# Pair attention: the second head of each pair is normalized on GpSimd, the first on VectorE

## The reference

```
s = q k^T / 8   (+ window mask and sink in layer 0)
p = exp(s - max) / sum(exp(s - max))
o = p v
```

## Time and profile before

| what | us |
|---|---|
| median of three runs | 2543.71 (2541.72 to 2549.36) |
| the profiled execution | 2542.04 |
| its span | 2540.2 |
| TensorE, matmul busy | 2137.8 (84%) |
| VectorE busy | 1087.4 (43%) |
| ScalarE busy | 681.5 (27%) |
| GpSimd busy | 262.3 (10%) |

### The profile page before, as it was taken

One profiled execution on the slowest core, in us unless ns is written; L12 is line 12 of the kernel. 1 busy time (PEld: TensorE's weight loads), 2 busy tenths in 40 slices (PEclk: granted clock), 3 DMA queues, 4 the chain that ended last, 5 costly groups with the idle time before them and its releaser, 6 DMA issues. The chain is left out here.

```text
span 2540.2 us, 29357 instructions
## 1 busy us (share of the span) xinstructions
PE 2137.8 (84%) x11338; PEld 1358.5 (53%) x11338; DVE 1087.4 (43%) x1713; ACT 681.5 (27%) x1048; POOL 262.3 (10%) x392
## 2 busy tenths in 40 slices
PE   6889999996999997987979888888568698888884
PEld 5777787784777876764733333333355433333331
DVE  5667644545676545467531111111576411111112
ACT  3343434332333432246211011111316111111111
POOL 2010000100000000000211111111120111111110
PEclk9989999997999998999979999999779799999997
DMA  8745565551655646310489999999810889999994
GB/s 278 266 144 203 181 211 191 202 200 67 236 199 182 217 173 216 110 35 1 189 354 396 409 413 406 410 404 382 276 25 1 311 356 408 422 415 413 413 414 188
DMA packets 175984, 655.24 MB, mean 258 GB/s; under 512 B 17680, under 2 KB 63200, under 8 KB 150544
## 3 DMA queue, kind: packets, MB, share of 16 engines
q1 hardware_dynamic: 157888, 618.45, 63.7%
q0 software_dynamic: 16752, 32.20, 3.9%
q10 hardware_dynamic: 1248, 3.25, 0.3%
HBM read 653.64 MB, written 21.17 MB: 266 GB/s over the span
## 5 line engine op out<-in xcount | busy, mean ns | idle before, releaser
L651 PE MATMUL bank<-sb_ring_rounded,sb_hT_rounded 128*128 128x512 f32 x2672 | 675.5, 397 | 18.9 <-DVE sb_hT_rounded L1727 12.2
L1185 PE MATMUL bank<-sb_ring,sb_arena 128*64 128x512 f32 x1984 | 507.4, 659 | 129.5 <-DMA sb_ring<-in_w_up 126.7
L651 PEld LDWEIGHTS bank<-sb_ring_rounded,sb_hT_rounded 128*128 128x128 f32 x2672 | 506.0, 191 | 128.5 <-DVE sb_hT_rounded L1727 14.1
L1740 DVE TENSOR_TENSOR sb_ring_rounded<-sb_ring,sb_ring_rounded 128x2048 fp32r<-128x2048 f32 (+1 forms) x148 | 328.2, 2259 | 133.1 <-ACT sb_ring_rounded L1295 132.8
L1185 PEld LDWEIGHTS bank<-sb_ring,sb_arena 128*64 128x64 f32 x1984 | 155.9, 150 | 426.4 <-issue 418.9
L1295 ACT ACTIVATE sb_ring_rounded<-sb_ring 128x2048 fp32r<-128x2048 f32 (+1 forms) x148 | 271.7, 1886 | 171.1 <-PE bank L651 141.8
L651 PE MATMUL bank<-sb_ring_rounded,sb_arena_rounded 128*128 128x512 f32 x1168 | 312.5, 393 | 2.0 <-DVE sb_arena_rounded L1727 1.0
L651 PEld LDWEIGHTS bank<-sb_ring_rounded,sb_arena_rounded 128*128 128x128 f32 x1168 | 221.1, 190 | 48.8 <-issue 2.6
L1209 PE MATMUL bank<-sb_ring,sb_arena 128*64 128x512 f32 x1024 | 233.7, 598 | 1.7 <-DVE sb_arena L2458 1.7
L1643 ACT ACTIVATE sb_hb<-bank 64x512 f32<-64x512 f32 x64 | 37.8, 590 | 644.6 <-PE bank L1185 644.6
L2458 DVE COPY sb_arena<-bank 128x256 f32<-128x256 f32 x64 | 27.2, 425 | 396.1 <-PE bank L1196 396.0
(11 more groups left out here) (315 smaller groups left out, 1955.0 us busy)
## 6 DMA issues: line engine op xcount, KB each, us to landing
sb_ring<-in_w_down SPq DMA_DIRECT2D x64, 2048.0 KB, 22.8
sb_ring<-in_w_up SPq DMA_DIRECT2D x62, 2048.0 KB, 21.8
sb_ring<-in_w_gate SPq DMA_DIRECT2D x62, 2048.0 KB, 17.5
sb_ring<-in_w_ada SPq DMA_DIRECT2D x48, 1024.0 KB, 7.4
sb_ring<-in_ffn_w_gu SPq DMA_DIRECT2D x44, 1024.0 KB, 7.7
sb_ring<-in_xa_w_kv SPq DMA_DIRECT2D x16, 1024.0 KB, 7.3
sb_ring<-in_ffn_w_down SPq DMA_DIRECT2D x16, 1024.0 KB, 6.4
sb_ring<-in_od_w_in SPq DMA_DIRECT2D x12, 1024.0 KB, 6.3
```

The costliest lines, as they stand in the source:

```text
L651: ins = pe.matmul(bank[b][0:rows, :], rnd(x), rnd(w[:, k, :]), start=start and k == k0 and q == 0, stop=stop and k == k1 - 1 and q == len( ...
L1185: ins = pe.matmul(bank[2 * j + part][part * ROWS:(part + 1) * ROWS, :], mxT[:, j, k, :], w[:, k, :], start=k == 0, stop=k == KD - 1)
L1740: dve.tensor_tensor(rnd(w), w, whole(high_of(n)[:, k0:k1, :]), ALU.subtract).then_inc(*c.up(s["w_lo"]))
```

## The change

VectorE inverts the sums as before, with a semaphore of its own (`inv_ready`), waits for its own result, and scales head 0 only, raising `p_ready`. GpSimd gets a loop over the same steps: it waits for `inv_ready`, scales head 1 in place and raises `p1_ready`. TensorE waits for both before the transposes of a pair. Two semaphores are added.

```diff
                         pe.wait_ge(*c.next(s["p_ready"]))
+                        pe.wait_ge(*c.next(s["p1_ready"]))
                         claim(T0)
...
-                        step(dve.reciprocal(inv, total))
-                        for a in range(2):
-                            e = j_e[:, m % 2, a, 0:nk]
-                            ins = dve.tensor_scalar(e, e, inv[:, a:a + 1], None, ALU.mult)
-                            if a == 0:
-                                ins.then_inc(*c.up(s["dve_step"]))
-                        ins.then_inc(*c.up(s["p_ready"]))
+                        dve.reciprocal(inv, total).then_inc(*c.up(s["inv_ready"]))
+                        dve.wait_ge(*c.last())
+                        e = j_e[:, m % 2, 0, 0:nk]
+                        dve.tensor_scalar(e, e, inv[:, 0:1], None, ALU.mult).then_inc(*c.up(s["p_ready"]))
...
+                for m, (t, i) in enumerate(pair_steps(l)):
+                    e, q = j_e[:, m % 2, 1, 0:len(key_tiles(t)) * P], 2 * (m % 2)
+                    pool.wait_ge(*c.next(s["inv_ready"]))
+                    pool.tensor_scalar(e, e, st[:, 29 + q:30 + q], None, ALU.mult).then_inc(*c.up(s["p1_ready"]))
                 tiles = 4 - 2 * l
                 pool.wait_ge(*c.next(s["o_split"]))
```

More of the change, by code:

```diff
@@ L175, in build_program @@
             "act_back", "act_go", "act_step", "ctx_loaded", "bcx", "o_split", "dve_step", "e_ready",
-            "es_ready", "fin_ready", "gla_dve", "h_ready", "idx_ready", "logits_read", "in_loaded",
+            "es_ready", "fin_ready", "gla_dve", "h_ready", "idx_ready", "inv_ready", "p1_ready", "logits_read", "in_loaded",
             "marks_ready", "fix_loaded", "mem_loaded", "mod_stored", "raw_stored0", "raw_stored1", "silu_ready", "ms_ready", "mul_ready", "nmax_ready", "out_done",
```

## The result

The changed kernel takes 2569.46 us (median of four runs, 2568.06 to 2576.57); the kernel before takes 2545.32 us beside it (four runs, 2541.72 to 2549.36). The ratio is 1.01, with a 95% interval of 1.0081 to 1.012: slower by 24.1 us. I had forecast 2545.8, with a range up to 2556.

What follows compares the result with a forecast made beforehand. A loop of waits between VectorE and TensorE in pair attention was taken to set the pace; +0.8 (layer 0, four tiles), +1.8 (layer 1) and -0.5 us (two tiles) gave +2.1, so 2545.8 us, range 2539 to 2556.

Steps and rivals of the forecast that it cites:

- the three stretches: Pair attention: layer 0 over four and two key tiles, layer 1 over four; 166 us where any microsecond reaches the end.
- the hold: GpSimd's scaling waits until VectorE's, taken as first, ends at 0.69 us after the reciprocal starts.
- d: Lateness of TensorE's transposes after the reciprocal's start: p - 0.53 = 0.37 us over four key tiles, 0.14 over two.
- VectorE's saving: One scaling fewer per VectorE iteration: 0.40 us over four key tiles, 0.27 over two, only where VectorE sets the iteration.
- halves of four tiles above 8.3 us: Sign of being wrong: two pairs over four key tiles taking longer than this; halves near 7.8 and 6.9 us were expected.
- p: GpSimd's time to scale one head of 128x512: 0.90 us, between 0.53 and 1.29 or 1.82; 0.54 for 256 columns.
- the rule quoted there: VectorE tensor_scalar in a two-port mode and GpSimd share ports; the first to issue keeps them for the whole instruction.
- 18p - 14.1: Total change in us over the pair attention as a function of GpSimd's price; +2.1 forecast, +9.1 at 1.29, +18.6 at 1.82.
- the clock: Rival: more TensorE idling brings one more part at 1.2 GHz, 1 to 3 us each; clock or something else 0.03.
- GpSimd slow: Rival, chance 0.16: GpSimd's price alone decides from 1.21 us on; 2552.8 us at 1.29, 2562.3 at 1.82.
- GpSimd first: Rival, chance 0.14: GpSimd's scaling gets hold first, VectorE's ends 0.36 us later; +8.4 us in all, 2552.1.
- No conflict: Rival, 0.12 together with a price near the lower bound: both scalings run at once; -3.2 us, 2540.5.

Runs made afterwards that it cites:

- two_sems: Against the changed kernel: VectorE scales both heads again, each with its own semaphore, TensorE waiting for both ahead of the transposes; 2545.86 us, stretches 108.31 and 58.86 us.
- pool_both: Against the changed kernel: GpSimd scales both heads, VectorE none; 2617.22 us in one execution, GpSimd's scaling 1.562 us for 512 columns.
- one_port: Against the changed kernel: VectorE scales head 0 in the slower form that also sums its row; 2574.16 us in one execution, GpSimd's scaling 1.566 us.
- between_dve: Against the kernel before: VectorE scales both heads, a semaphore each, TensorE's wait for head 1 between the two heads' transposes; 2541.68 us, ratio 0.9982.

## Why the prediction was wrong

**Right:** the place and the mechanism. The time went into the three stretches. VectorE came first, its scaling unchanged; the handover left GpSimd's record 0.06 us behind it; the hold was 0.29 us (0.31 in the sum: the 0.44 left of VectorE's scaling less 0.13). The second wait costs nothing, as two_sems shows. In the settled halves, those at the lower clock apart, d is added to the loop's half to 0.1 us, and VectorE's saving is worth 0.20 us in the one half over two tiles that it sets, and nothing over four. I had named halves of four tiles above 8.3 us as a sign of being wrong; they are 8.47.

**Wrong:** the term p. "One input read and one output written lies between the write-only and the two-input row; I take the middle, p = 0.90 us". Measured by itself it is 1.565 us for 512 columns and 0.925 for 256. It is more than the two-input row makes with a fixed part (1.29), so the order in which I had put the three kinds was wrong, and the middle had nothing to stand on. Why this scaling costs more than the operation on two inputs would at that width, no run shows. The Trainium skill's 769 ns for 512 elements (GPSIMD Engine Reference, section 3.1) is for a best case; against this operation it is half of what was measured. The true value lay between my own upper bounds of 1.29 and 1.82; the range left out the higher one. The lower bound was also worked out wrongly: 1.823 us over 2048 columns is 0.89 ns a column, or 0.80 beyond a fixed 0.18 us, and gives 0.59 us and not 0.53. That moves the middle by 0.03 us and decides nothing.

A reading of the earlier trace rows was too strong. The prediction says that the trace agrees at both places with the rule quoted there. But at 508.50 VectorE runs a tensor_tensor and not a tensor_scalar, and at 1267.01 the engine recorded first was the one held. The two places show that one engine can hold the other, not that the first one does.

With p = 1.565 my line 18p - 14.1 gives +14.1 us. Measured at equal clock it is 16.2; the sum's other terms are good to some 2 us. The line would have given a median of 2557.8. The 11.7 us that are missing to 2569.46 are these 2, about 5 of the clock, 1.6 by which the kernel before has a higher median beside it than alone (2545.32 against 2543.71), and 3 that stay open with the parts outside the stretches. These parts rest on few traces; only the first 14.1 are worked out from the loop.

**Too small:** the clock. "More idle could bring one more such part, at 1 to 3 us each" stood under the rivals with 0.03. It is some 5 us on average. It goes with the lateness, though not in every execution: in layer 0 the granted clock was 0.91, 0.94 and 0.88 in the three traces of the changed kernel, 0.94, 0.94 and 0.98 in those of the kernel before, and 0.80 in pool_both, where the transposes are latest. Why equal executions differ in it is open.

So the rival *GpSimd slow*, with a chance of 0.16, was what happened, though its price is 1.565, and with that price the loop gives 2557.8; of the rest, which carried the median beyond even that rival's upper end of 2562.3, the lower clock is the largest part that I can name. *GpSimd first* did not occur; forced, it gave something else than it said. *No conflict* is refuted by the hold that one_port takes away.

## What to carry to other kernels

When an operation inside a loop of waits goes to another engine, count from the moment the inputs are ready to the moment the consumer can go on; that VectorE becomes free sooner is worth nothing if it waits in the same loop. A price that the trace does not show is not to be interpolated between rows of other operations: let the range reach both bounds, or give the rival at the upper bound more chance. If the second half of a pair is late, put the wait for it between the halves: with both on VectorE, that was the only part of this change that gained (between_dve, 4.2 us). Delaying the value products as well came out as fast, not measurably faster.

## What the hardware showed that was unexpected

- GpSimd's scaling by a per-partition value, 128x512, takes 1.565 us alone, VectorE's 0.486; per column 2.5 ns against 0.52. GpSimd's operation on two inputs in the earlier trace rows would have led to less: 454 ns over 128 columns, where this one would come to 0.28 + 0.32 = 0.60.
- Between these two scalings the conflict is not symmetric. Behind VectorE's fast scaling GpSimd is held until it ends (0.29 us). Behind GpSimd's, VectorE is slowed to 0.838 us but ends 0.6 us before it. A memset on GpSimd did hold VectorE to its end (2.05 us for 64 columns).
- Two fast VectorE scalings in a row with GpSimd beside them take 1.32 us in place of 0.88, and GpSimd 1.784 in place of 1.565: it gets in between the two.
- The same instructions took 116.1 or 123.5 us in layer 0, with a granted clock of 0.94 or 0.88. Waits that a change adds can be paid twice: as waits, and as more time of TensorE at its lower level.
